# Expert weights that arrive as two halves of 4 KB rows, read and returned by halves

## The reference

```python
def expert_block(args):
    xblk, e = args
    hid = jax.nn.silu(xblk @ w_gate[e]) * (xblk @ w_up[e])
    return hid @ w_down[e]
```

## Time and profile before

| | before |
|---|---|
| median of 3 runs | 2505.9 us (2502.89 to 2506.16) |
| profiled execution, time | 2506.82 us |
| profiled execution, span | 2505.0 us |
| TensorE busy | 2416.0 us, 96% |
| DMA, mean over the span | 283 GB/s |
| ring loads of gate, up, down | 128, 128, 108 of 1 MB |

### The profile page before, as it was taken

One profiled execution on the slowest core, in us unless ns is written; L12 is line 12 of the kernel. 1 busy time (PEld: TensorE's weight loads), 2 busy tenths in 40 slices (PEclk: granted clock), 3 DMA queues, 4 the chain that ended last, 5 costly groups with the idle time before them and its releaser, 6 DMA issues.

```text
span 2505.0 us, 37491 instructions
## 1 busy us (share of the span) xinstructions
PE 2416.0 (96%) x14914; PEld 1737.9 (69%) x14915; DVE 1423.6 (57%) x2520; ACT 909.9 (36%) x1610; POOL 310.7 (12%) x377
## 2 busy tenths in 40 slices
PE   7999999998999999998899999999999999999998
PEld 4664444443785444443588899988888889998887
DVE  6563333232775333332466786676676678666667
ACT  3541111110333111111244475554444447544443
POOL 0210001000000001000000123430010012244001
PEclk9989999999998999999999999999999999999999
DMA  9999999999888999999946554444644755444471
GB/s 397 368 387 408 420 419 419 417 419 420 289 331 354 419 420 419 419 419 419 371 164 231 173 176 152 142 141 163 230 167 158 246 181 186 135 140 148 136 268 51
DMA packets 245426, 708.85 MB, mean 283 GB/s; under 512 B 11266, under 2 KB 163458, under 8 KB 189186
## 3 DMA queue, kind: packets, MB, share of 16 engines
q1 hardware_dynamic: 244818, 705.54, 74.0%
q10 hardware_dynamic: 432, 0.88, 0.1%
HBM read 705.33 MB, written 1.05 MB: 282 GB/s over the span
## 4 chain that ended last, share of the span: by engine, by line
PE 75%; DMA 11%; DVE 6%; issue 3%; ACT 3%; POOL 1%; SPq 0%; DVEq 0%; ACTq 0%; POOLq 0%
PE w L1424 14%; PE y L1178 11%; PE w L1171 11%; DMA ring<-in_e_w_up_dram 10%; PE w L1096 8%; PE w L1442 7%; PE w L1170 5%; PE w L1099 4%; DVE wsp L1816 2%; PE y L1478 2%; PE w L1371 2%; PE y L972 1%; ACT wsp L1806 1%; ACT arena L3084 1%; DMA ring<-in_ada_w_dram 1%
## 5 line engine op out<-in xcount | busy, mean ns | idle before, releaser
L1816 DVE TENSOR_TENSOR wsp<-ring,wsp 128x1024 fp32r<-128x1024 f32 x452 | 559.4, 1247 | 278.1 <-ACT wsp L1806 277.1
L1806 ACT CAST wsp<-ring 128x1024 fp32r<-128x1024 f32 x452 | 468.4, 1048 | 260.8 <-PE w L1171 97.9
L1424 PE MATMUL w<-ring,arena 128*64 128x512 f32 x2048 | 461.6, 599 | 38.1 <-DMA ring<-in_e_w_up_dram 38.1
L1424 PEld LDWEIGHTS w<-ring,arena 128*64 128x64 f32 x2048 | 147.9, 137 | 304.6 <-issue 298.0
L1171 PE MATMUL w<-hx,wsp 128*128 128x512 f32 x1344 | 348.1, 391 | 0.0
L1171 PEld LDWEIGHTS w<-hx,wsp 128*128 128x128 f32 x1344 | 246.9, 189 | 44.3
L1096 PE MATMUL w<-hx,wsp 128*128 128x256 f32 x1984 | 263.2, 285 | 2.4 <-ACT arena L3048 1.7
L1096 PEld LDWEIGHTS w<-hx,wsp 128*128 128x128 f32 x1984 | 245.8, 191 | 15.0 <-issue 8.1
L1178 PE MATMUL y<-wsp,zsp 128*128 128x512 f32 x1008 | 245.5, 392 | 3.9 <-DVE wsp L1816 2.2
L2957 ACT ACTIVATE ht<-w 128x256 f32<-128x256 f32 x64 | 40.1, 626 | 573.2 <-PE w L1424 573.2
L2391 DVE TENSOR_TENSOR ht<-w,ht 128x256 f32<-128x256 f32 x64 | 39.5, 618 | 354.8 <-ACT ht L2957 354.8
(11 more groups left out here) (380 smaller groups left out, 2967.9 us busy)
## 6 DMA issues: line engine op xcount, KB each, us to landing
ring<-in_e_w_gate_dram SPq DMA_DIRECT2D x128, 1024.0 KB, 13.4
ring<-in_e_w_up_dram SPq DMA_DIRECT2D x128, 1024.0 KB, 14.6
ring<-in_e_w_down_dram SPq DMA_DIRECT2D x108, 1024.0 KB, 13.4
ring<-in_ffn_in_dram SPq DMA_DIRECT2D x88, 1024.0 KB, 7.0
ring<-in_ada_w_dram SPq DMA_DIRECT2D x48, 1024.0 KB, 13.4
ring<-in_w_in_dram SPq DMA_DIRECT2D x48, 1024.0 KB, 5.3
ring<-in_ffn_out_dram SPq DMA_DIRECT2D x44, 1024.0 KB, 7.1
ring<-in_b_w_in_dram SPq DMA_DIRECT2D x12, 1024.0 KB, 10.3
```

Source lines behind the costliest of these rows:

```text
L1424: ins = pe.matmul(b[64 * c:64 * c + 64, :], xg[:, u, kc, x0:x0 + CAP], r4[:, k, :, 256 * c:256 * c + 256], start=kc == 0, stop=kc == KC - 1)
L1806: ac.copy(shaped(halves(i)[0], u.shape), u.cut(ring[:, u.piece % NSLOT, :])).then_inc(*mark("w_high", i))
L1816: ve.tensor_tensor(shaped(lo, u.shape), u.cut(ring[:, u.piece % NSLOT, :]), shaped(hi, u.shape).bitcast(F32), ALU.subtract).then_inc(*mark ...
```

## The change

In the mixtures a ring piece whose predecessor in the same slot was also an expert piece is loaded by two DMAs instead of one: numbers 0 to 1023 of each partition, and then numbers 1024 to 2047. Each partition's run is then 4 KB instead of 8 KB. The first half raises a new semaphore (`half0` to `half3`, one for a pair of slots), the second half the slot's own. TensorE waits for the first halves before row blocks 0 and 1, and for the whole pieces before row blocks 2 and 3; it raises `ring_read` once more after the first two. `down` does likewise with its two chunks of a piece. The new block in `sync_engine` stands behind the waits that were there.

```diff
@@ sync_engine
                     else:
                         sp.wait_ge(*at("ring_read", pieces[n - NSLOT].get("read", n - NSLOT)))
+                if n >= NSLOT and "halves" in piece and "halves" in pieces[n - NSLOT]:
+                    rows, room = piece["halves"], ring[:, n % NSLOT, :]
+                    sp.wait_ge(*at("ring_read", pieces[n - NSLOT].get("read", n - NSLOT), "half"))
+                    sp.dma_start(room[:, 0:1024], rows[:, 0:1024]).then_inc(*mark(f"half{n % NSLOT // 2}", n, by=16))
+                    sp.wait_ge(*at("ring_read", pieces[n - NSLOT].get("read", n - NSLOT)))
+                    sp.dma_start(room[:, 1024:2048], rows[:, 1024:2048]).then_inc(*mark(f"ring{n % NSLOT}", n, by=16))
...
+                    continue
@@ up
                         for v in range(2):
                             np_ = piece_of["up", l, e_, 2 * h + v]
-                            pe.wait_ge(*at(f"ring{np_ % NSLOT}", np_))
+                            first_half(np_)
...
                         for k in range(4):
                             kc = 4 * h + k
+                            if k == 2:
+                                ins.then_inc(*mark("ring_read", np_, "half"))
+                                for v in range(2):
+                                    whole_piece(np_ - 1 + v)
...
+                def in_halves(n_):
+
+                    return n_ >= NSLOT and "halves" in pieces[n_ - NSLOT]
+
+                def first_half(n_):
+
+                    pe.wait_ge(*(at(f"half{n_ % NSLOT // 2}", n_ | 1) if in_halves(n_) else at(f"ring{n_ % NSLOT}", n_)))
+
+                def whole_piece(n_):
+
+                    if in_halves(n_):
+                        pe.wait_ge(*at(f"ring{n_ % NSLOT}", n_))
@@ down
-                            pe.wait_ge(*at(f"ring{np_ % NSLOT}", np_))
+                            first_half(np_)
                             w = whole(ring[:, np_ % NSLOT, :])
                         for c in range(2):
+                            if c == 1 and e_ not in ONCE:
+                                ins.then_inc(*mark("ring_read", np_, "half"))
+                                whole_piece(np_)
```

More of the change, by code:

```diff
@@ L663, in program @@
                 pieces.append({"parts": [(lambda r: r, src.rearrange("(p k) n -> p (k n)", p=P))], "units": [],
-                               "read": len(pieces) + 1 - u})
+                               "read": len(pieces) + 1 - u, "halves": src.rearrange("(p k) n -> p (k n)", p=P)})
             elif w[0] == "down":
@@ L670, in program @@
                 piece_of[w] = len(pieces)
-                pieces.append({"parts": [(lambda r: r, src.rearrange("(p k) n -> p (k n)", p=P))], "units": []})
+                pieces.append({"parts": [(lambda r: r, src.rearrange("(p k) n -> p (k n)", p=P))], "units": [],
+                               "halves": src.rearrange("(p k) n -> p (k n)", p=P)})
         assert len(units) == len(unit_list)
@@ L944, in sync_engine @@
                         sp.wait_ge(*at("ring_read", pieces[n - NSLOT].get("read", n - NSLOT)))
+                if n >= NSLOT and "halves" in piece and "halves" in pieces[n - NSLOT]:
[4 more added lines that the diff above has]
+                    sp.dma_start(room[:, 1024:2048], rows[:, 1024:2048]).then_inc(*mark(f"ring{n % NSLOT}", n, by=16))
+                    for l in range(DEPTH):
+                        if n == piece_of["down", l, E - 1, 1] and not sig.blank:
+                            late(l)
+                    continue
                 for view, src in piece["parts"]:
```

## The result

The changed kernel takes 2528.29 us (median of 4 runs, 2524.71 to 2529.69), the kernel before 2504.39 us (median of 4 runs, 2502.14 to 2506.16). The two medians lie 23.9 us apart. The ratio is put at 1.0089, with a 95% interval from 1.0076 to 1.0102, which is 22 us slower, between 19 and 26. The forecast was 19 us, and 2525 us in a range from 2510 to 2537.

What follows compares the result with a forecast made beforehand. The prediction took the mixtures to be bound by the DMA load rate, 419 GB/s. Bytes 16.1, small packets 3.2, dry moments -0.9 and TensorE's side 0.6 gave 19.0 us on 2505.9, so 2524.9 us, range 2510 to 2537.

Steps and rivals of the forecast that it cites:

- The bound: In both mixtures the DMA engines are always busy, share 1.01 at 419 GB/s, and TensorE follows the loads.
- The bytes: 348 mixture pieces in 4 KB runs at 411.4 GB/s, 0.046 us more each, 16.1 us in all.
- the stretches with 4 KB runs: Five short stretches elsewhere in this kernel, 400 to 422 GB/s, length-weighted mean 411.4, taken as the rate of halved pieces.
- The line through 1 KB and 8 KB packets: A fit with 37.9 ns per KB and 9.3 ns per packet, giving 407 GB/s for 4 KB packets.
- The second small packet: Each halved piece's second DMA brings each engine one more semaphore packet, 9.3 ns, 3.2 us over 348 pieces.
- The dry moments: Holes early in the mixtures where late slots leave the engines without work; slower transfers fill them, giving back 0.9 us.
- TensorE's side: At each mixture's end `up` finishes 1.2 us sooner, but `down` waits for both first halves; 0.6 us added over both.
- The sum: All terms over the whole kernel: 16.1 + 3.2 - 0.9 + 0.6 = 19.0 us slower.
- No loss of rate: Rival: 4 KB runs in the mixtures move as fast as 8 KB runs, 2503 to 2507 us; chance 0.10.
- the faster case: Rival: mixtures bound by the way from slot to piece, so TensorE's 32 waits could go, down to 2468 us; chance 0.06.
- TensorE did not become the bound: Rival claimed it would, through 1.4 us waits before `down` in 54 experts, 2544 us; chance 0.04.
- The most costly case: Rival: halved pieces run at the lowest stretch's 400 GB/s, 44 us slower in all, 2550 us; chance 0.06.

Runs made afterwards that it cites:

- the experiment with one DMA: Kernel before, but the 348 expert pieces are read in 4 KB runs by one 1 MB DMA each; 2527.24 us against 2505.73, ratio 1.0085.
- real_release: Changed kernel without the old wait ahead of the new block, so a first half is issued once the old first half is read; 2528.4 us, ratio 1.0089.
- whole_waits: Changed kernel's loads, but TensorE waits for whole pieces as in the kernel before; 2528.04 us, ratio 1.0092.
- down_whole: Changed kernel, but `down` waits for whole pieces, each for its own, instead of first halves of both; 2527.05 us, ratio 1.0087.
- every_other_partition: Kernel before, but each of the 348 pieces is loaded by two DMAs, even and odd partitions, in 8 KB runs; 2509.7 us against 2506.22, ratio 1.0015.

## Why the prediction was right, point by point

- *The bound.* That the mixtures are bound by the rate of the loads stood on the earlier trace rows. Every kernel that kept the engines busy moved with that rate: 418 GB/s cost 3.5 us, 408 cost 21.5, 386 and 383 cost 71.
- *The bytes.* 16.1 us by the mean of the stretches with 4 KB runs, 411.4 GB/s. It was 408 to 409, and the experiment with one DMA puts the term at 21.5 us. Right in kind, 5 us too small, and below the 18 us at which that experiment's interval starts. This is the weak point that the prediction itself named: short stretches beside other traffic stood for a full queue. The line through 1 KB and 8 KB packets gave 407 GB/s and would have been 25.5 us, so the truth lay between the two views. The figure that the prediction named from the Trainium skill (DMA: Bandwidth & Descriptors, section "iDMA fabric"), 408.7 GB/s, agrees with the 408 to 409 measured here.
- *The second small packet.* 3.2 us, with nothing as its lower bound. Measured with runs of 8 KB: 3.5 us, between 1.5 and 6. That run has the second DMA and its small packets together, so it does not show that the packet is what costs.
- *The dry moments.* 0.9 us given back. This is below what the times resolve, but the hole of the first mixture is closed in the changed kernel (share 1.02 from 210 to 220 us, where the one before had 0.74 in half of it). That the change releases nothing early was read from the order of waits, and in `real_release` a release by halves did not help either.
- *TensorE's side.* 0.6 us for both mixtures. The wait of 1.47 us before the last `down` is in the trace. The waits for loads, put at 57 us, were 61.9: 38.1 and the 23.5 us that the mixtures lost make 61.6. `whole_waits` and `down_whole` show that where these waits stand makes no difference that can be measured in the times.
- *The sum.* 19.0 us against 22 (23.9 by the medians). Nearly all of the error is in the first term: with the measured 21.5 and 3.5 in place of 16.1 and 3.2 the sum is 24.7 us, inside the interval from 19 to 26. Packets were put at 295538 with 16834 small ones; the page has 295543 and 16834. The mixtures' ends were put at 9 to 10 and at 19 us, and came 9.6 and 20.7 us later. The first of these hits is luck: without the lead of 2.8 us ahead of the first mixture it would have been 12.4. That nothing changes behind the mixtures did not hold for the profiled pair, by 2.8 us.
- *The rivals.* No loss of rate and the faster case fell with the 409 GB/s. TensorE did not become the bound: in `whole_waits`, with no wait for halves before `down`, the time stayed. The most costly case, 400 GB/s, did not come in a full queue.

## What to carry to other kernels

Where the DMA engines are busy throughout, count packets before anything else: here each more packet of an engine cost 8 ns, which is 2.5% in going from 8 KB to 4 KB runs and 8% in going to 2 KB, and neither an earlier start nor, behind one queue in order, an earlier release of the buffer paid for it. Cut a load by halves only where the engines have room, and check that the queue that issues the loads does not wait for the whole before it comes to the half. Longer runs did not pay here. With 16 KB runs the buffers came back in larger pieces and the loads ran dry, so look at that before counting the packets saved; no run here had the longer runs alone.

## What was not expected of the hardware

A DMA that writes partitions 0 to 63 and one that writes 64 to 127 together moved 251 to 277 GB/s, at a busy share of 0.93 to 1.02, while the same bytes with even and odd partitions moved 418. Shown is only that it goes with which partitions one DMA covers. The reason that the expectation of `every_other_partition` gave fits both runs, but neither run measures it. The kernel took 575 us more, some 25 times the change itself, with a lower clock of TensorE as a part of it.

A float32 matmul whose moving columns come as pairs with a stride of 4 took 612 ns instead of 592, and a whole `up` of them 7.42 us instead of 7.09.
